# First two attention units of layer 1 scored ahead of the projection's last gate tile, and that tile's SiLU finished later on VectorE

## The reference, cut to what matters

```python
z = rmsnorm(x) @ w_in                      # 1024 -> 2864 columns
q, kc, vc, ks, vs, kw, vw, gate, bgate = split_cols(z)
q, ks, kw = rmsnorm_heads(q), rmsnorm_heads(ks), rmsnorm_heads(kw)
gates = sigmoid(bgate)                     # 16 heads x 3 branches
# per head: compressed blocks, selected blocks, window
o = gates[..., 0] * o_cmp + gates[..., 1] * o_sel + gates[..., 2] * o_win
y = x + (o * silu(gate)) @ w_out
```

## Time and profile before

| | |
|---|---|
| Median of 3 runs | 962.53 us (960.93 to 965.6) |
| Profiled execution | 960.3 us |
| Its span, first to last instruction | 958.7 us |
| PE busy | 911.0 us, 95% of the span |
| DVE busy | 480.1 us, 50% |
| ACT busy | 293.2 us, 31% |
| POOL busy | 249.2 us, 26% |
| PE share of the chain that ended last | 84% |
| Mean granted TensorE clock | 0.985 of full |

### The profile page before, as it was taken

How to read it: one execution, slowest core, us unless ns; L and a number is a source line. 1 busy time by engine, 2 the same in 40 slices (tenths; PEclk the granted TensorE clock), 3 DMA queues, 4 the chain that set the end, 5 groups by cost and what they waited for, 6 DMA issues and landing times.

```text
span 958.7 us, 15899 instructions
## 1 busy us (share of the span) xinstructions
PE 911.0 (95%) x5224; PEld 484.8 (51%) x5224; DVE 480.1 (50%) x965; ACT 293.2 (31%) x716; POOL 249.2 (26%) x353
## 2 busy tenths in 40 slices
PE   8999999999899999999999999998899998887998
PEld 4444444444455553545565676566554444444444
DVE  1248777779344643212133262724677775776211
ACT  6111111103454541032101110433565564655000
POOL 0000223200033430340424242000443354357000
PEclk9999999999999999999999999999899997999999
DMA  9333666593154457782414142030122232033211
GB/s 356 105 126 119 226 226 192 189 287 79 45 147 158 138 193 271 255 195 91 135 42 146 34 143 87 13 90 12 42 60 66 65 94 97 1 92 108 92 45 45
DMA packets 82487, 117.61 MB, mean 123 GB/s; under 512 B 21006, under 2 KB 45790, under 8 KB 82094
## 3 DMA queue, kind: packets, MB, share of 16 engines
q1 hardware_dynamic: 61824, 78.87, 25.2%
q0 software_dynamic: 10944, 29.41, 10.4%
q10 hardware_dynamic: 9648, 8.41, 2.7%
HBM read 108.70 MB, written 11.36 MB: 125 GB/s over the span
## 4 chain that ended last, share of the span: by engine, by line
PE 84%; DVE 6%; DMA 3%; ACT 3%; issue 2%; POOL 1%; POOLq 1%; SPq 0%; ACTq 0%; DVEq 0%
PE ps L729 26%; PE ps L989 11%; PE ps L995 6%; PE ps L1293 6%; PE ps L1012 4%; PE ps L738 4%; PE ps L1051 3%; PE ps L927 3%; PE ps L1163 3%; PE ps L1174 3%; DMA arena<-cache_sb_v 2%; PE ps L905 2%; DVE work L2000 2%; PE ps L877 2%; PE ps L1029 1%
## 5 line engine op out<-in xcount | busy, mean ns | idle before, releaser
L729 PE MATMUL ps<-wring,arena 128*128 128x512 f32 x448 | 195.3, 594 | 1.5 <-issue 1.5
L729 PEld LDWEIGHTS ps<-wring,arena 128*128 128x128 f32 x448 | 84.1, 190 | 104.0 <-issue 103.9
L668 POOL TENSOR_TENSOR z<-z,work 128x1024 f32<-128x1024 f32 (+1 forms) x64 | 80.1, 1254 | 159.6 <-DVE work L2008 159.3
L989 PE MATMUL ps<-wring,z 128*128 128x512 f32 (+2 forms) x320 | 106.7, 488 | 0.0
L1525 ACT ACTIVATE z<-ps,work 128x512 f32<-128x512 f32 (+3 forms) x128 | 66.4, 525 | 72.0 <-DVE work L2000 69.8
L1348 ACT ACTIVATE z<-ps 128x512 f32<-128x512 f32 (+1 forms) x64 | 27.4, 433 | 181.8 <-PE ps L729 147.5
L360 POOL DMA_DIRECT2D arena<-cache_sb_k x64 | 34.4, 537 | 164.1 <-DVE work L1643 141.6
L989 PEld LDWEIGHTS ps<-wring,z 128*128 128x128 f32 x320 | 54.8, 190 | 43.4 <-issue 41.8
L1848 DVE TENSOR_TENSOR arena<-ps,consts 128x512 f32<-128x512 f32 x32 | 30.3, 1020 | 82.3 <-PE ps L1029 82.3
L1805 DVE TENSOR_TENSOR xres<-xres,ps 128x512 f32<-128x512 f32 (+1 forms) x32 | 15.5, 484 | 86.4 <-PE ps L1293 38.9
L1012 PE MATMUL ps<-arena,wring 64*128 64x512 f32 (+3 forms) x256 | 54.3, 502 | 4.2 <-ACT z L1525 4.2
(11 more groups left out here) (322 smaller groups left out, 1272.5 us busy)
## 6 DMA issues: line engine op xcount, KB each, us to landing
wring<-w_in SPq DMA_DIRECT2D x12, 2048.0 KB, 11.1
arena<-cache_sb_k POOLq DMA_DIRECT2D x64, 256.0 KB, 3.1
arena<-cache_sb_v SPq DMA_DIRECT2D x64, 256.0 KB, 3.7
wring<-w_out SPq DMA_DIRECT2D x3, 2048.0 KB, 7.9
arena<-cache_sel_k SPq DMA_DIRECT2D x64, 64.0 KB, 1.8
consts<-aux SPq DMA_DIRECT2D x1, 2315.5 KB, 15.1
xres<-x_prompt SPq DMA_DIRECT2D x4, 512.0 KB, 8.0
wring<-w_in SPq DMA_DIRECT2D x2, 1024.0 KB, 7.1
```

The costliest lines, as they stand in the source:

```text
L668: nc.gpsimd.tensor_tensor(P_u(n), P_u(n), bc(coef(n).unsqueeze(2), [P, 2, (NT - n % NT) * P]), ALU.mult).then_inc(n_scaled, 1)
L729: mm = pe.matmul(ps[:, t, 0:width], stat, mov, start=(k == 0), stop=(k == KT - 1))
L989: mm = pe.matmul(ps[:, bank, at:at + w], normed1(k, t), wring[:, slot, k, lo:lo + w], start=(k == 0), stop=(k == KT - 1))
```

## The change

In the last chunk the order of the steps is turned round: steps 0 and 1 are now the branch gates, with the sample rows right behind step 1; steps 2 and 3 are the gate tiles 6 and 7, both in bank 4, so that step 2 waits for the eviction of the sample rows and step 3 for that of step 2. `turn_q(0)` moves from `s` = 22 to `s` = 21, its copy on ACT with it. `scores(0)` and `scores(1)` stand at `s` = 22, ahead of `turn_keys(1)` and of step 3. ACT does `exp(0)` and `exp(1)` behind its part of `s` = 22, ahead of the eviction of step 3; DVE does `row_max(0)`, `row_max(1)` and `gate_weight(0)` behind its own part of `s` = 22. The weights of units 0 and 1 go to a free stretch of `spare`.

Sigmoid is no longer evaluated on ACT: it writes `exp(-x)` for the branch gates, and DVE adds 1 and takes the reciprocal (192 columns, then 48 for the sample rows) at `s` = 22. Tile 7 is evicted twice, as `exp(-x)` into `gate_exp` and as a plain copy, and DVE finishes its SiLU in loop step 12: add 1, reciprocal, multiply, 512 columns each.

```diff
+        gate_exp = z[:, NT, P_OFF:P_OFF + CH]
             def P_u(n):
-                return z[:, n % 4, P_OFF:P_OFF + 2 * (NT - n % NT) * P].rearrange("p (u n) -> p u n", u=2)
+                w = 2 * (NT - n % NT) * P
+                a = spare[:, n * 2 * CH:n * 2 * CH + w] if n < 2 else z[:, n % 4, P_OFF:P_OFF + w]
+                return a.rearrange("p (u n) -> p u n", u=2)
 # SP
-                sp.wait_ge(bank_free, 5 + 80)
+                sp.wait_ge(heads_ready, 3)
 # PE, between(s): s == 21
+                        turn_q(0)
                     if s == 22:
+                        pe.wait_ge(bank_free, 5 + 5 * 15 + 2)
+                        scores(0)
+                        scores(1)
                         turn_keys(1)
...
-                    if s == 22:
-                        turn_q(0)
-                    if s == 23:
-                        pe.wait_ge(bank_free, 5 + 5 * 15 + 2)
-                        scores(0)
 # PE, chunks
-                        pe.wait_ge(bank_free, n * 5 + (t + 1))
+                        pe.wait_ge(bank_free, n * 5 + ((t + 1) if c < 5 or t < 2 else NT + 2 + t))
...
-                        elif c == 5 and t >= 2:
-                            by_tokens(slot, t, 2 * t - 4, 2 * P, 3 * HN, 0)
-                            mm = by_tokens(slot, t, 2 * t - 3, 2 * P, 3 * HN, 3 * HN)
+                        elif c == 5 and t < 2:
+                            by_tokens(slot, t, 2 * t, 2 * P, 3 * HN, 0)
+                            mm = by_tokens(slot, t, 2 * t + 1, 2 * P, 3 * HN, 3 * HN)
+                        elif c == 5:
+                            mm = by_gates(slot, NT, (t - 2) * P)
...
+                        if c == 5 and t == 1:
+                            project_rows(n, slot, xnT_ready, 5, W1 - c * CH, lhs=normed1_rows)
                         between(4 * c + t)
...
-                pe.wait_ge(bank_free, 5 + 5 * 15 + NT)
-                scores(1)
                 pe.wait_ge(bank_free, 5 + 80)
                 pe.wait_ge(kz_ready, 3)
 # ACT, fetch(21)
+                        act.wait_ge(nq_turned, 1)
+                        nc.scalar.activation(qTs[:, 0], ps[:, 7, :], ACT.Copy, scale=SCALE).then_inc(nq_T, 1)
 # ACT, chunks
+                        elif c == 5 and t < 2:
+                            ins_ = nc.scalar.activation(z[:, pair, BG:W1], ps[:, t, 0:2 * 3 * HN].rearrange("p (t c) -> p t c", t=2), ACT.Exp, scale=-1.0)
+                        elif c == 5 and t == 3:
+                            nc.scalar.activation(gate_exp, ps[:, NT, :], ACT.Exp, scale=-1.0)
+                            ins_ = nc.scalar.activation(gateT(7), ps[:, NT, :], ACT.Copy)
+                        elif c == 5:
+                            ins_ = nc.scalar.activation(gateT(6), ps[:, NT, :], ACT.Silu)
...
+                        if c == 5 and t == 1:
+                            evict_rows(c, [(2 * P, 2 * P + 3 * HN, ACT.Exp, -1.0), (0, 2 * P, ACT.Silu, 1.0)])
                         fetch(4 * c + t)
+                        if c == 5 and t == 2:
+                            nc.scalar.preload_act_table_set(LOG_EXP)
+                            exp(0)
+                            exp(1)
 # DVE, between(22)
+                        dve.wait_ge(bank_free, 5 + 5 * 15 + 3)
+                        for g in (z[:, 0:NT, BG:W1], z[0:NB, NT, BG:W1]):
+                            st.done(TS(g, g, 1.0, None, ALU.add))
+                            rec = nc.vector.reciprocal(g, g)
+                            rec.then_inc(heads_ready, 1) if g.shape[0] == NB else st.done(rec)
 # DVE, chunks
                 for s in range(4 * NC1):
                     between(s)
+                    if s == 4 * NC1 - 2:
+                        row_max(0)
+                        row_max(1)
+                        gate_weight(0)
 # DVE, units (the three calls above stood right ahead of this loop)
+                    if n == 12:
+                        dve.wait_ge(bank_free, 5 + 80)
+                        st.done(TS(gate_exp, gate_exp, 1.0, None, ALU.add))
+                        st.done(nc.vector.reciprocal(gate_exp, gate_exp))
+                        st.done(TT(gateT(7), gateT(7), gate_exp, ALU.mult))
```

More of the change, by code:

```diff
@@ L1477, in fetch @@
                         nc.scalar.activation(cvT[:, HB:N_CMP], ps[:, 7, 0:HN1], ACT.Copy).then_inc(cvT_ready, 1)
-                    if s == 22:
-                        act.wait_ge(nq_turned, 1)
-                        nc.scalar.activation(qTs[:, 0], ps[:, 7, :], ACT.Copy, scale=SCALE).then_inc(nq_T, 1)
                     if s == 21:
@@ L1526, in exp, with evict_rows @@
                                              accum_out=dens(n)[:, u:u + 1]).then_inc(n_p, 1)
+                def evict_rows(c, parts):
+                    act.wait_ge(mm_done, 5 * (10 + c) + (3 if c == 5 else NT + 1))
+                    for a, e, f, scale in parts:
+                        for row, a2, e2 in quarters(a, e):
+                            ins_ = nc.scalar.activation(z[0:NB, NT, c * CH + a2:c * CH + e2], ps[row:row + NB, NT, 0:e2 - a2], f, scale=scale)
+                    ins_.then_inc(bank_free, 1)
@@ new lines, in _ @@
+                for c in range(NC1):
+                    n = 10 + c
+                    for t in range(NT):
+                        act.wait_ge(mm_done, 5 * n + t + (2 if c == 5 and t >= 2 else 1))
+                        pair = slice(2 * (t % 2), 2 * (t % 2) + 2)
+                        if c < 3:
+                            ins_ = nc.scalar.activation(z[:, t, c * CH:(c + 1) * CH], ps[:, t, :], ACT.Copy)
+                        elif c == 3 and t < 2:
+                            ins_ = nc.scalar.activation(z[:, pair, KW:GATE], ps[:, t, :].rearrange("p (t c) -> p t c", t=2), ACT.Copy)
+                        elif c == 5 and t < 2:
[5 more added lines that the diff above has]
+                            ins_ = nc.scalar.activation(gateT(6), ps[:, NT, :], ACT.Silu)
+                        else:
+                            ins_ = nc.scalar.activation(gateT(t + (-2, 2)[c - 3]), ps[:, t, :], ACT.Silu)
+                        ins_.then_inc(bank_free, 1)
+                        if c == 5 and t == 1:
+                            evict_rows(c, [(2 * P, 2 * P + 3 * HN, ACT.Exp, -1.0), (0, 2 * P, ACT.Silu, 1.0)])
+                        fetch(4 * c + t)
+                        if c == 5 and t == 2:
+                            nc.scalar.preload_act_table_set(LOG_EXP)
+                            exp(0)
+                            exp(1)
+                    if c == 3:
+                        evict_rows(c, [(0, 2 * P, ACT.Copy, 1.0), (2 * P, CH, ACT.Silu, 1.0)])
+                    elif c < 5:
+                        evict_rows(c, [(0, CH, ACT.Silu if c == 4 else ACT.Copy, 1.0)])
@@ L1528, in copy_p, with q_copy @@
+                def q_copy(i):
+                    act.wait_ge(nq_turned, i + 1)
+                    act.wait_ge(n_s, 8 * (i - 1)) if i > 1 else None
+                    act.wait_ge(nc_s, i - 1) if i > 1 else None
+                    nc.scalar.activation(qTs[:, i % 2], ps[:, 7, :], ACT.Copy, scale=SCALE).then_inc(nq_T, 1)
                 def copy_p(n):
@@ L1546, in _ @@
                 load_window("cache_win_k", 0, kset[2], cm_turned, 4 * NB, sk_loaded[2])
-                exp(0)
-                exp(1)
                 for n in range(NUNIT):
@@ L1981, in between @@
                         nc.vector.tensor_copy(o_cmp, ps[:, 5, 0:P]).then_inc(*marks_dve.next("i_out"))
[L1983 to L1990, removed]
                 def row_max(n):
@@ L2008, in gate_weight @@
                     TT(coef(n), dens(n), gates, ALU.mult).then_inc(n_c, 1)
+                for s in range(4 * NC1):
+                    between(s)
+                    if s == 4 * NC1 - 2:
+                        row_max(0)
+                        row_max(1)
+                        gate_weight(0)
+                dve.wait_ge(mm_done, 5 * 15)
+                nc.vector.memset(HALF2[:, 1024:1536], 0.0).then_inc(kz_ready, 1)
+                dve.wait_ge(kz_ready, 3)
+                pc = p_cmp[:, :, :, 0:NPB]
+                cs = small[:, 0:8].rearrange("p (t u) -> p t u", t=NT)
                 def cmp_max(i):
@@ L2083, in mix @@
                     TT(gateT(i), gateT(i), ps[:, 6, :], ALU.mult).then_inc(n_mix, 1)
-                row_max(0)
-                row_max(1)
-                gate_weight(0)
                 for n in range(NUNIT):
```

3 lines of the change are left out of this document (2 added, 1 removed).

## The result

The changed kernel takes 965.15 us (median of 22 runs, 961.37 to 969.63), the kernel before 961.85 us in runs beside it (22 runs, 959.18 to 965.6). The ratio is 1.0030, with a 95% interval of 1.0017 to 1.0042: 2.9 us slower, between 1.6 and 4.0 (the two medians are 3.3 apart). The profiled execution took 965.27 us, its span 963.6.

The account below looks back on a forecast made before the run. PE, busy 95% of the span, was taken as the bound. Front gain -1.9, step-12 wait +4.06 and clock +2.4 gave +4.6 us, forecast 967 on the median's scale, range 961 to 970.5.

Parts of the forecast that it names:

- case A: Whole kernel: front gain of 1.9 us, new DVE wait 4.06 and half clock 2.4 give +4.6 us, 967; chance 0.50.
- B: Rival: waits as summed but a milder clock, no fall upon tile 6 or none behind step 12; 963 to 965.5; chance 0.22.
- The two waits in front: Ahead of the loop: PE waits for DVE 0.76 us before `turn_q(0)` and 1.94 us before `scores(2)`.
- The eviction of the sample rows at no cost: Ahead of tile 6: PE's work and wait cover ACT's 2.07 us eviction, costed at nothing; 2.07 without that cover.
- The clock in front: Ahead of the loop: 1.7 us of half-clock loss removed, and one fall of 1.7 us expected again upon tile 6.
- the narrow fall: Half clock after PE's 48-column products, priced at 1.7 us; bounds 0 (no fall) and 3.4 (one behind each pair).
- the half clock of the opening: First loop steps, up to 678.0: hidden behind DVE, which sets the pace; DVE's chain shortens by only 0.45 us.
- Gain kept: Ahead of the loop: 3.6 us gained less 1.7 for the clock leaves 1.9 us, with ends at 3.6 and 0.2.
- The reciprocal: DVE, loop step 12, 512 columns: 4.24 us at 8.0 ns a column, making the block 5.47 and PE's wait 4.06.
- The clock behind that wait: PE after its new 4.06 us wait: half clock costs 2.4 us, bounds 0 and 4.9.
- C: Rival: cheap reciprocal of 0.68 us in step 12, PE waits 0.5, clock stays; 959.4 to 961.1, not slower; chance 0.16.
- E: Rival: loop opening follows PE, not DVE, winning up to 3.0 us more, with a cheap block; near -6, 956.5; chance 0.04.

## Why the prediction was right, and where it was off

**The direction and the order of size: right.** The forecast was +4.6 us, and +2.9 came, by the mechanism of case A: a gain in front, and more than that lost behind the late SiLU. Two of its terms were too large, so that the time, 965.15, within the stated 961 to 970.5, fell just under the range that A gave itself (965.5 to 969.5), into that of B. Of the 1.85 us between 967 and 965.15, 0.7 are the base: the forecast was added to 962.53, a median of three runs, where 22 runs gave 961.85. Luck has a part too: the front won 0.6 less than forecast, which made up for some of what the reciprocal was put too high.

**The two waits in front: right.** 0.75 for 0.76, and 1.97 for 1.94. Both were read from DVE's and PE's rows of before, and the releasers are the ones named. `scores(2)`, counted from the start of the last chunk (627.81 before, 630.89 after), comes 44.21 - 41.32 = 2.89 us earlier, for 3.17.

**The eviction of the sample rows at no cost: right.** It took 2.06 us, and ACT's timeline has 0.01 us ahead of the table load and 0.02 between its end and the next pass (649.41 + 1.28 to 650.71). A drain, which the Trainium skill counts beside the load ("ScalarE: Activation LUTs", "What ACT_TABLE_LOAD costs"), does not show. The cover named for it was there, and thin: with the wait of `turn_q(0)` gone, 0.35 us of it came out.

**The clock in front: near in sum, by luck, and wrong in its parts.** The forecast counted the narrow fall of 1.7 us as removed, and charged one again upon tile 6. The fall at 661 belonged to one execution. It's in one of four profiles of the old order: in the second of before, the `scores(0)` products take 1.13 us, where the first had 1.47.

```profile
663.32 1.13 PE L1012 MATMUL ps<-arena,wring 64*128 64x512 f32 x4
```

In the new order it came in three of nine profiles, and not upon tile 6 but on the sample rows: these took 3.25 us at half clock in the second profile without the late SiLU, 1.92 in after's.

```profile
646.60 3.25 PE L741 MATMUL ps<-wring,z 128*8 128x128 f32 x48
```

Since the forecast took it once on each side, it cancelled. Not foreseen was the half clock from 673 to 680 behind the new wait of 1.97. The forecast took the half clock of the opening as hidden behind DVE's chain. PE's next two turns into bank 7 show how far that held, first before, then the first of them after (its second, at 683.36, stands above):

```profile
678.35 0.63 PE L1206 MATMUL ps<-consts,arena 128*128 128x128 f32 x4
...
682.76 0.66 PE L1002 MATMUL ps<-consts,z 128*128 128x128 f32 x4 [1.49 <-DVE wring L2032]
```

```profile
678.08 1.09 PE L1211 MATMUL ps<-consts,arena 128*128 128x128 f32 x4
```

At the first turn 3.35 us are won (47.19 for 50.54 from the start of the last chunk), 0.46 of them behind `scores(2)`, for the 0.45 of the forecast. But the half clock lasted on to 680, and at the turn at 683.36 only 2.48 are left: 0.9 us of it came out. Gain kept: 2.5 us in after's profile against before's, of which 1.3 is the fall that before's first execution had and its other three profiles had not; 1.3 as a mean of the profiles, for 1.9.

**The reciprocal: the term that was mis-sized.** 3.35 us for 4.24. The block took 4.53 for 5.47, and the wait was 2.86 for 4.06; of the missing 1.20, 0.94 is the block, and 0.21 is that `row_max(15)` to the end of the copy took 1.82 us (720.41 to 722.23) and not 2.03, since behind a late block its parts no longer wait in between. The slope of 8.0 ns a column was read between 2 and 8 columns. Those two rows are 48 ns apart, and a few ns in either are carried 85 times over on the way to 512. With 128, 192 and 512 columns (0.95, 1.35, 3.35 us) the slope is 6.25 ns, twice over, and about 0.15 us remains as a fixed part. The Trainium skill ("VectorE: DVE Perf Modes", "First, the fixed hardware budget") tells of 8 repeats, from which the prediction estimated 4.27. At the 0.96 GHz of that estimate, 6.25 ns are 6 cycles a column. Here the measurement decides.

**The clock behind that wait: within its bounds, too high.** 0 in after's profile and 1.6 us in the one with the block in the kernel before, for 2.4. The rule behind the 2.4, that waits of 2.71 us and more were followed by half clock and one of 2.21 was not, was read from one execution and did not hold (see the last section). For the 0.8 us that A's lower end put in this place no row was named.

**The sum again,** with what was measured: -1.3 + 3.03 + (0 to 1.6) = +1.7 to +3.3 us, which the ratio's 2.9 (1.6 to 4.0) agrees with; the differences ahead of the change are not in it. Of the rivals, B, with a chance of 0.22, gives these numbers (+2.2 to +2.9), but it kept the wait at 4.06: what came is a smaller wait as well as a milder clock. C needed a reciprocal below 2.1 us, E an opening that DVE doesn't set.

## What to carry to other kernels

Work that is put off into a loop has to fit the slack of the engine that takes it, in one piece: look up which of its instructions stand behind it and who waits for them, then cut it (four pieces cost 1.2 us by the trace, the block 3.0) or give it to the engine that has the time (two more ACT passes of 0.63 us replaced 3.8 us of DVE). A price read from two small shapes gives the fixed part of an instruction; it doesn't give its rate, so keep both ends. And a fall of the clock that one profile has, or lacks, is a property of that execution until a second one shows it.

## What was not expected of the hardware

The same wait is followed by different clocks. Waits of 2.86 us in the same place and from the same releaser had 3.4 us at half clock behind them in one kernel and none in another; waits of 3.97 to 3.98 us at 258 had 3.4 or 6.8 us, each time the same in three profiles of one kernel. Even the shorter wait of 1.97 us had 6.8 us at half clock behind it. The prediction's line between 2.21 us (no fall) and 2.71 us (a fall) does not hold at its own wait either: in all twelve other profiles PE's wait for the same DMA, 2.06 to 2.42 us, has 3.4 us at half clock right behind it, and only the execution that the prediction was read from has none. In after's profile:

```profile
856.10 0.86 PE L1245 MATMUL ps<-consts,wring 128*32 128x128 f32 x24 [2.25 <-DMA consts<-cache_sel_v]
```

```profile
858.00:858.50 0.50, 0.50 (x3) 0.50 0.00 0
```
